# A third k-pair by seven products in iterations 5 to 8 of block 2's up projection, and one pair in iteration 9

## The reference

```python
def swiglu(h, w_in, w_down):
    gu = h @ w_in
    gate, up = jnp.split(gu, 2, axis=-1)
    return (jax.nn.silu(gate) * up) @ w_down

x = x + swiglu(rmsnorm(x, norm_ffn_g[layer]), w_ffn_in[layer], w_ffn_down[layer])
```

## Time and profile before

| what | us |
|---|---|
| median of 3 runs | 2559.72 (2559.7 to 2560.38) |
| the profiled execution | 2560.11 |
| its span | 2558.3 |
| PE busy | 2548.7 |
| DVE busy | 1799.7 |
| ACT busy | 1372.3 |

### The profile page before, as it was taken

One profiled execution on the slowest core, in us unless ns is written; L12 is line 12 of the kernel. 1 busy time (PEld: TensorE's weight loads), 2 busy tenths in 40 slices (PEclk: granted clock), 3 DMA queues, 4 the chain that ended last, 5 costly groups with the idle time before them and its releaser, 6 DMA issues.

```text
span 2558.3 us, 33757 instructions
## 1 busy us (share of the span) xinstructions
PE 2548.7 (100%) x12362; PEld 2122.1 (83%) x12362; DVE 1799.7 (70%) x2203; ACT 1372.3 (54%) x1754; POOL 99.7 (4%) x110
## 2 busy tenths in 40 slices
PE   9999999999999999999999999999999999999998
PEld 8887788888888888888887888888888888888887
DVE  6656656877777788885767665456578988747888
ACT  5455545666555554555645466444555555445454
POOL 2000000111111100000000000000000000000000
PEclk9999999999999999999999999999999999999999
DMA  7745565666666576656655555665666666667664
GB/s 243 219 151 157 164 186 175 211 207 207 189 189 188 180 269 199 224 182 195 181 175 163 160 149 156 196 191 182 187 197 206 216 210 195 200 189 257 202 215 163
DMA packets 281438, 494.09 MB, mean 193 GB/s; under 512 B 14578, under 2 KB 123236, under 8 KB 281056
## 3 DMA queue, kind: packets, MB, share of 16 engines
q1 hardware_dynamic: 277952, 478.73, 60.3%
q0 software_dynamic: 3184, 13.41, 1.5%
q10 hardware_dynamic: 176, 0.27, 0.0%
HBM read 483.17 MB, written 9.18 MB: 192 GB/s over the span
## 4 chain that ended last, share of the span: by engine, by line
PE 98%; DVE 1%; ACT 0%; issue 0%; DVEq 0%; ACTq 0%
PE acc L829 18%; PE acc L831 18%; PE acc L830 18%; PE acc L1129 13%; PE acc L1122 7%; PE tp L1173 3%; PE tp L1175 3%; PE tp L1174 3%; PE acc L1173 3%; PE acc L1175 3%; PE acc L1174 3%; PE tp L857 1%; PE tp L920 1%; PE tp L1415 1%; PE tp L1416 1%; PE tp L1417 1%
## 5 line engine op out<-in xcount | busy, mean ns | idle before, releaser
L2088 DVE TENSOR_TENSOR WL<-WR,WH 128x1024 fp32r<-128x1024 f32 x680 | 841.9, 1241 | 577.0 <-ACT WH L1495 574.9
L1495 ACT ACTIVATE WH<-WR 128x1024 fp32r<-128x1024 f32 x680 | 719.1, 1059 | 759.6 <-PE acc L831 585.2
L829 PE MATMUL acc<-WH,A 128*128 128x512 f32 x1200 | 474.0, 395 | 0.1
L831 PE MATMUL acc<-WH,A 128*128 128x512 f32 x1200 | 467.7, 390 | 0.0
L830 PE MATMUL acc<-WL,A 128*128 128x512 f32 x1200 | 467.3, 389 | 0.0
L1129 PE MATMUL acc<-A,WH 128*128 128x512 f32 x1408 | 336.4, 391 | 0.0
L1129 PEld LDWEIGHTS acc<-A,WH 128*128 128x128 f32 x1408 | 258.6, 188 | 50.0
L829 PEld LDWEIGHTS acc<-WH,A 128*128 128x128 f32 x1200 | 225.3, 188 | 48.8 <-issue 3.6
L831 PEld LDWEIGHTS acc<-WH,A 128*128 128x128 f32 x1200 | 225.2, 188 | 48.0
L830 PEld LDWEIGHTS acc<-WL,A 128*128 128x128 f32 x1200 | 225.5, 188 | 44.8
L829 PE MATMUL acc<-WH,XH 128*128 128x512 f32 x544 | 216.4, 398 | 0.0
(11 more groups left out here) (441 smaller groups left out, 3513.8 us busy)
## 6 DMA issues: line engine op xcount, KB each, us to landing
WR<-in_w_in_dram SPq DMA_DIRECT2D x199, 512.0 KB, 3.8
WR<-in_w_ffn_up_dram SPq DMA_DIRECT2D x176, 512.0 KB, 3.6
RAW<-in_w_ffn_down_dram SPq DMA_DIRECT2D x88, 1024.0 KB, 5.0
WR<-in_w_ffn_in_dram SPq DMA_DIRECT2D x176, 512.0 KB, 3.9
WR<-in_w_out_dram SPq DMA_DIRECT2D x64, 512.0 KB, 3.6
WR<-in_w_in_dram SPq DMA_DIRECT2D x65, 256.0 KB, 3.0
WR<-in_w_ple_gate_dram SPq DMA_DIRECT2D x32, 512.0 KB, 4.1
WR<-in_w_branch_a_dram SPq DMA_DIRECT2D x16, 512.0 KB, 3.8
```

The source lines that it names most:

```text
L829: pe.matmul(o, H[:, kt + k, cols], WH[:, s, k], start=begin, stop=False)
L831: mm = pe.matmul(o, L[:, kt + k, cols], WH[:, s, k], start=False, stop=end)
L1495: act.activation(WH[:, n % RING], WR[:, n % RING], ACT.Copy).then_inc(hi_done, 1)
L2088: dve.tensor_tensor(WL[:, n % RING], WR[:, n % RING], WH[:, n % RING].bitcast(F32), ALU.subtract).then_inc(lo_done, 1)
```

## The change

The table of pairs now names them. Iterations 5 to 8 have a third pair, (0, 2) with (1, 2), at place 12, and iteration 9 has that pair alone, at place 4. PE issues 15 matmuls fewer. Iteration 0 makes the sums of x for the third pair (five sums or differences and one remainder on DVE, one rounding on ACT, each half the size of the same step for the first two pairs together). The orders of ACT and DVE follow the places.

```diff
-UP_SEVENS = (0, 2, 2, 2, 2, 2, 2, 2, 2, 0, 0)
+UP_PAIRS = ((), (0, 1), (0, 1), (0, 1), (0, 1), (0, 1, 2), (0, 1, 2), (0, 1, 2), (0, 1, 2), (2,), ())
+UP_SEVENS = [len(js) for js in UP_PAIRS]
...
+    return gate[:4] + pairs[0] + gate[4:] + up[:1] + pairs[1] + up[1:3] + pairs[2] + up[3:]
...
-    return [i for i in (4, 8) if i // 4 <= UP_SEVENS[it]]
+    return [4, 8, 12][:UP_SEVENS[it]]
...
-    return (8, 9, 11)[UP_SEVENS[it]]
+    return (8, 9, 11, 14)[UP_SEVENS[it]]
...
-                    if i - RING in sevens_of(it):
-                        k = sevens_ahead(it) + sevens_of(it).index(i - RING)
+                    back, place = (it, i - RING) if i >= RING else (it - 1, i + 16 - RING)
+                    if back >= 0 and place in sevens_of(back):
+                        k = sevens_ahead(back) + sevens_of(back).index(place)
                         sp.wait_ge(q_sum, UP_SUMMED + ACT_STEPS + 3 * k + 3)
...
+                copy_at, silu_at = ((None, 11), (9, 13), (13, 15), (17, 18))[UP_SEVENS[it]]
+                for i in range(8, 20):
+                    if i in places:
+                        hi_pair(base + i)
+                        hi_sums(sevens_ahead(it) + places.index(i))
+                    elif i - 1 not in places:
+                        split([i])
+                    if i == copy_at:
+                        copy_up_p1(it)
+                    if i == silu_at:
+                        silu_of_gate(it)
...
+                places, sums_at = sevens_of(it), (None, 12, 13, 17)[UP_SEVENS[it]]
+                for i in range(8, 20):
+                    if i in places:
+                        k = sevens_ahead(it) + places.index(i)
+                        lo_pair(base + i)
+                        sums_of_blocks(base + i, k)
+                        lo_sums(k)
+                    elif i - 1 not in places:
+                        split([i])
+                    if i == sums_at:
+                        gate_sums(it)
...
+                    if i == 18 and UP_SEVENS[it] == 3:
+                        gated_h(it)
+                if UP_SEVENS[it] < 3:
+                    gated_h(it)
```

More of the change, by code:

```diff
@@ L232, in turned_bank @@
     return 2 if any(UP_SEVENS[it + 1:it + 2]) else 0
-ACT_STEPS = 5
+ACT_STEPS = 10
 SLOTS, ENTRIES = 11, 3
@@ L240 @@
 ORDERS = [order_of(pattern, range(SUM_J), range(SUM_J, PER_HALF)) for pattern in (EARLY, LATE)]
-UP_BETWEEN = (sum(UP_SEVENS), 1 + 2 * sum(UP_SEVENS), ACT_STEPS + 3 * sum(UP_SEVENS), 1 + 2 * sum(UP_SEVENS))
+UP_BETWEEN = (sum(UP_SEVENS), 2 + 2 * sum(UP_SEVENS), ACT_STEPS + 3 * sum(UP_SEVENS), 2 + 2 * sum(UP_SEVENS))
 QUADS = quads(((0, (ORDERS[1], ORDERS[0]), lambda n: (0, 0, 1)[n] if n < 3 else (0, 2, 1)[n % 3], True),
@@ L827, in chunk @@
                         o, s = into[:, a, tb, :] if into is acc else into[:, tb, :], n % RING
-                        begin, end = first and k == 0, last and k == CHUNK_KT - 1
+                        begin, end = first and k == 0, pair(last, tb) and k == CHUNK_KT - 1
                         pe.matmul(o, H[:, kt + k, cols], WH[:, s, k], start=begin, stop=False)
@@ L1407, in _, with gate_up_seven @@
             tile(AH, AL, KT, C_UP2, 8, 1, A_UP2[1])
-            def gate_up_seven(it, i, j, k, opens, ends):
+            def gate_up_seven(it, i, j, k, opens, ends, closes):
                 n, cols = C_UP2 + 16 * it + i, [slice(tb * P, (tb + 1) * P) for tb in range(TB)]
@@ L1423, in summed @@
                     at = slice(m * P, (m + 1) * P)
-                    return product(o, ASH[:, j, at], ASL[:, j, at], h, l, begin, end)
+                    high, low = (ASH[:, j, at], ASL[:, j, at]) if j < 2 else (ASH2[:, 0, at], ASL2[:, 0, at])
+                    return product(o, high, low, h, l, begin, end)
                 pe.wait_ge(lo_done, n + 2)
                 raw(tp[:, 0, :], 2 * j, 0, wh[:, 2], wl[:, 2], opens, ends)
-                summed(acc[:, 0, 0, :], 2, wh[:, 1], wl[:, 1], False, False)
+                summed(acc[:, 0, 0, :], 2, wh[:, 1], wl[:, 1], False, closes)
                 if opens:
@@ L1442, in with_sevens @@
                 order, places, turn_last = up_order(it), sevens_of(it), turn_h(it - 1, it == 1)
+                last = [max(i for i, (b, j) in enumerate(order) if b == a and j not in UP_PAIRS[it]) for a in range(2)]
                 pe.wait_ge(acc_free[0], A_UP2[0] + it)
@@ L1446, in with_sevens @@
                         s = places.index(i)
-                        gate_up_seven(it, i, j, sevens_ahead(it) + s, s == 0, i == places[-1])
+                        gate_up_seven(it, i, j, sevens_ahead(it) + s, s == 0, i == places[-1],
+                                      i == places[-1] and i > last[0])
                     elif i - 1 not in places:
-                        chunk(AH, AL, 2 * j, C_UP2 + 16 * it, i, a, i == 0, i == (gate_whole(it) - 1, 15)[a])
+                        chunk(AH, AL, 2 * j, C_UP2 + 16 * it, i, a, i == 0,
+                              (i == last[a] and (a or i > places[-1]), i == last[a]))
                     turn_last(i)
@@ L2003, in up2 @@
                 base, places = C_UP2 + 16 * it, sevens_of(it)
[L2004 to L2025, removed]
+                copy_at, silu_at = ((None, 11), (9, 13), (13, 15), (17, 18))[UP_SEVENS[it]]
[9 more added lines that the diff above has]
+                        silu_of_gate(it)
+                    if it == 0 and i in (13, 17):
+                        high, whole = ((ASH, ASF), (ASH2, ASF2))[i // 17]
+                        act.wait_ge(q_sum, UP_SUMMED + (5, 10)[i // 17])
+                        act.activation(high[:], whole[:], ACT.Copy).then_inc(q_hi, 1)
                 if UP_SEVENS[it + 1]:
```

71 lines of the change are left out of this document (31 added, 40 removed).

## The result

The changed kernel takes 2569.09 us in the median of 7 runs (2565.74 to 2570.13), the kernel before in the same comparison 2560.08 (2559.70 to 2562.13): a ratio of 1.0033, 95% interval 1.0024 to 1.0043. The change costs 9.0 us where 5.5 were forecast. The profiled execution took 2570.13 us, with a span of 2568.4, 10.1 us more than that of the kernel before.

What follows compares the result with a forecast made beforehand. PE, 100% busy, was taken to bound the kernel. Waits of 8.9 us less 3.4 us of matmuls gave 5.5 us slower: 2565.6 against the profiled 2560.11, with the median 0.4 lower at 2565.2 us; range 2561.5 to 2570.5.

Steps and rivals of the forecast that it cites:

- 15 matmuls, 3.40 us: PE, iterations 5 to 9: five pairs newly made by seven drop 15 matmuls of 0.2267 us, gaining 3.40 us.
- As a load, all of it is hidden; iteration 0 costs nothing: DVE at 39.1 of 42.4 us and ACT at 23.7 still fit; iteration 0's 2.7 us of sums are hidden.
- PE waits for the silu at four starts: Starts of iterations 6 to 9: three successive loads, then additions and silu, hold PE 1.6 to 3.3 us each.
- rival A: Starts of iterations 6 to 9: loads hidden, ACT's copy sets the wait, 1.1 us each; +1.0 to +3, 2561.7; chance 0.15.
- Waits of 3.3, 1.6, 1.85 and 2.15 us, 8.9 in all: PE's waits after iterations 5, 6, 7 and 8, from iteration 6's carried-on rows, adjusted for each chain start.
- The start of the chain: ACT's rounding at place 8: varies by iteration, with 0.3 us coming back from iteration 6 on.
- the growth from iteration to iteration: Place 8's rounding starts later through iterations 6, 7 and 8 (14.48, 14.72, 15.03 us in), making waits 1.6, 1.85, 2.15 us.
- terms for late landings: Upper end: two later load landings, 1.1 us for each of four iterations, plus 0.5 for the first: +11.
- The granted clock stays at 2.4 GHz: PE throughout: the forecast kept clock 1.00 and put no clock cost in its sum.
- a clock of 0.50 after a stall: Sign of being wrong: PE's granted clock at 0.50 following a wait.
- its 43.9 to 45.7: Sign of being right: iterations of 43.9 to 45.7 us instead of 43.05, iteration 9 of 43.7.
- rival D: PE's clock falls: one chunk after each of four stalls at 1.2 GHz, 10.9 us more, 2576; chance 0.03.

Runs made afterwards that it cites:

- e4: Changed kernel with iterations 5 to 8 back at two pairs, keeping iteration 9's pair and iteration 0's sums: 2559.62 us, -0.7 against the kernel before.
- e10: Changed kernel with PE released after the fifth addition, and copy and additions behind chunk 16's split; second chip: 2557.17 us, -3.5 against the kernel before.
- e7: e6 with the third pair from iteration 1 on, so in iterations 1 to 4 too: 2566.59 us, +6.0 against the kernel before.
- e2: Changed kernel with PE released after the fifth addition, not the silu, following three-pair iterations: 2558.81 us, -1.5 against the kernel before.
- e5: Changed kernel with ACT's copy and DVE's six additions behind the split of chunk 16, not 17: 2563.08 us, +2.5 against the kernel before.
- e3: Changed kernel with eight never-read matmuls before PE's wait at the start of iterations 6 to 9: 2566.27 us, +6.0 against the kernel before.
- e8: Changed kernel with the six additions behind the split of chunk 18, not 17: 2588.04 us, +27.5 against the kernel before.
- e6: Changed kernel with PE released after the fifth addition, and copy and additions behind chunk 16's split; first chip: 2558.01 us, -2.6 against the kernel before.

## Why the prediction was right

Step by step, as it was put:

- *15 matmuls, 3.40 us.* Right. e4 has 3 of them (-0.7 us), e10 all (-3.5).
- *As a load, all of it is hidden; iteration 0 costs nothing.* Right here (e4, e10), and the limit is near (e7).
- *PE waits for the silu at four starts, since chunk 17's load, rounding and split come late and the additions and the silu follow.* Right, in place, number and order. The largest wait is the one at iteration 6, the loads of 16 go out at the end of the third pair's sums (2138.80 against 2138.77), and iteration 9 takes 43.77 us. e2 takes away the end of that chain, e5 its middle, and e5's last three waits sit on the floor worked out for rival A, 1.15 us against 1.1.
- *Waits of 3.3, 1.6, 1.85 and 2.15 us, 8.9 in all.* Measured 3.3, 2.2, 2.4 and 2.4, in all 10.3: the iteration lengths less the 42.4 us of e10, less 1.6 where the clock fell. The mis-sized terms are the landings: the loads of 12 and 13 came 0.15, 0.26 and 0.27 us later than the row they were taken from in iterations 6 to 8, those of 16 and 17 0.06, 0.16 and 0.26, and the additions took 0.10 longer each time. The start of the chain was forecast 0.3 us sooner than before; from PE's transpositions to ACT's rounding at place 8 it was 9.01, 9.00 and 8.94 us, where 8.74, 8.99 and 9.26 follow from the forecast. So the growth from iteration to iteration did not come, and only the sum of these three starts was right. (The 0.3 us that the earlier split of the pair at place 4 gives did come: from the transpositions to that split it is 2114.61 - 2112.74 = 1.87 us, before 2110.74 - 2108.58 = 2.16.) One slip of the sum: its terms for late landings, 4.4 + 0.5 us over 5.5, make +10.4, which is what 2570.5 stands for, and not +11.
- *The granted clock stays at 2.4 GHz.* This is the step that failed, and the prediction's own list has "a clock of 0.50 after a stall" among the signs of being wrong; two iterations, of 47.3 and 46.4 us, lie outside its 43.9 to 45.7 for that reason. It was rival D, with a chance of 0.03 and a price of one chunk at 1.2 GHz, 2.72 us, behind each of four waits; it was 1.6 us behind two. In the profiled execution the clock fell behind two of the four waits and cost 3.2 us. e3 fills the waits, has no fall and is 3.0 us faster, though part of that may be shorter waits; e8 has the fall behind every wait. The mean clock of six of the seven timed runs is 0.998 and they took 2568.9 to 2570.1 us; the seventh has 0.999 and took 2565.74. Without the 3.2 us the forecast of 2565.2 would have stood within 0.7 us, in part by chance: the waits were 1.4 us too short in it, and the median lay 1.0 us under the profiled execution where 0.4 was forecast. The reason given against it, that no row of before shows the other level, said only that PE never stood there: it was no evidence about a kernel in which PE does. The Trainium skill (TensorE: Matmul & The Clock Gate, "HAM oscillation") tells of waits for loads that throttled the array each time; e8's trace agrees (four waits of 5.6 us, four falls), the changed kernel's in two of its four shorter waits.

So the sum of 5.5 us was too small by 1.4 us of waits and by the clock's 3.2; of the profiled execution's 10.1 us the median shows 9.0. The direction and the waits were understood. That the time lies in the range is partly luck: the upper end had been opened for late loads, and what filled it was mostly the clock, which the sum had put at nothing.

What stays open: what, beside its length, decides whether a wait of 2 to 3 us lets the clock fall. It fell after 3.3 and 2.4 us and not after 2.2 and 2.4 of the same execution. Nor is it known why the loads land 0.1 to 0.3 us earlier or later. From the transpositions to the rounding at place 8 it is 8.94 to 9.01 us in the changed kernel, 8.84 to 8.97 in e5 and 8.72 to 9.00 in e8. The one kernel that was profiled twice, on two chips, had 10.42 to 10.55 us (e6) and 9.95 to 10.36 us (e10), so as much can come from the chip or from chance.

## What to carry to other kernels

Where a full engine waits at a stage's border, count the time from the last operand to the release of the border, not the loads of the helpers: here both helpers fit, and what mattered was how many chunks stood behind the last pair. Release a buffer when its last reader has read it, not when the result made from it is finished; that edit alone went from 9.0 us slower than before to 1.5 us faster. And add to every new wait of 2 us or more of a TensorE that was busy throughout the chance that it comes back at half its clock; here it did so behind two of four waits of 2.2 to 3.3 us, and cost 1.6 us each time.

## What was not expected of the hardware

- Waits of PE that lost 2.2 to 3.3 us sometimes, and waits of 5.6 us always, were followed by a stretch at a granted clock of 0.50. The stretch begins with the restart (e8) or up to 1.3 us behind it (2241.29 to 2242.55), so PE may start at full speed and slow down then.
- With the waits filled by matmuls that nobody reads the clock was 1.00 throughout, and the kernel was 3.0 us faster for 32 matmuls more.
- The same kernel (e6, e10) differed by 0.9 us from one chip to another in its difference to the kernel before, and by 0.1 to 0.4 us in three of its iterations: that much of a margin in a chain of loads can come and go.
